# Two decoder blocks on one Trainium2 core: stores of the gate products put in front of the weight loads, reloaded products split earlier, one wait on the last gate narrowed

## The reference

```python
def swiglu_ffn(h, w_in, w_out):
    gate, up = jnp.split(h @ w_in, 2, axis=-1)
    return (jax.nn.silu(gate) * up) @ w_out

# in second_block, FFN_HIDDEN = 2816 = 22 x 128:
h = rms_norm_2(x, pre2_w[l]) * (1.0 + sc2) + sh2
y = swiglu_ffn(h, ffn_w_in[l], ffn_w_out[l])
x = x + (1.0 + gt2) * rms_norm_2(y, post2_w[l])
```

## Time and profile before

| | |
|---|---|
| median of three runs | 2207.89 us (2206.18 to 2208.21) |
| the profiled execution's own time | 2202.16 us |
| its span, first to last instruction | 2200.4 us |
| mean granted clock of TensorE | 0.995 of full speed |
| PE busy | 2147.3 us (98%) |
| POOL, DVE, ACT busy | 1178.6, 1149.8, 710.2 us |
| gate stage | about 1492 to 1632 us of the span |
| unit stage | about 1632 to 1938 us |
| down stage | about 1941 to 2185 us |

### The profile page before, as it was taken

The page is one execution under the profiler, slowest core; times in us unless marked ns, Lnnn a source line. Parts: engine busy times, 40 slices in busy tenths (PEclk is TensorE's granted clock), DMA queues, the critical chain, the costliest instruction groups (busy, mean ns, idle before and its releaser), DMA issues.

```text
span 2200.4 us, 29316 instructions
## 1 busy us (share of the span) xinstructions
PE 2147.3 (98%) x11096; PEld 1743.1 (79%) x11096; DVE 1149.8 (52%) x1413; ACT 710.2 (32%) x878; POOL 1178.6 (54%) x1096
## 2 busy tenths in 40 slices
PE   7999999999999999999999999999999999999997
PEld 5778887887777877787888888887778887878886
DVE  7988873367543261361597246545563343444307
ACT  6663342335433242121222331234432222312112
POOL 3342224566652232222585344566578887857776
PEclk9999999999999999999999999999999999999999
DMA  6224414232421111112233244433754444445343
GB/s 231 87 106 172 172 62 142 73 106 86 162 78 38 68 41 65 55 42 77 87 133 115 97 142 143 162 108 133 261 188 159 151 156 173 174 158 182 134 153 125
DMA packets 93601, 275.16 MB, mean 125 GB/s; under 512 B 8512, under 2 KB 19008, under 8 KB 93504
## 3 DMA queue, kind: packets, MB, share of 16 engines
q1 hardware_dynamic: 81152, 254.97, 32.9%
q10 hardware_dynamic: 12352, 18.88, 2.3%
HBM read 221.38 MB, written 52.43 MB: 124 GB/s over the span
## 4 chain that ended last, share of the span: by engine, by line
PE 85%; DVE 5%; ACT 3%; DMA 2%; issue 1%; DVEq 1%; SPq 1%; POOL 1%; POOLq 1%; ACTq 0%
PE PG L820 37%; PE PG L826 18%; PE PG L1407 13%; PE PG L1321 6%; PE PX L820 2%; PE PX L826 1%; DMA p_gates<-PGB 1%; PE PX L1050 1%; PE PX L1045 1%; PE PG L921 1%; DVE WK L2214 1%; PE PX L1028 1%; PE PX L1065 1%; DVE PX L2220 1%; PE PX L998 0%
## 5 line engine op out<-in xcount | busy, mean ns | idle before, releaser
L820 PE MATMUL PG<-UL,WH 128*128 128x512 f32 x1696 | 662.0, 390 | 0.0
L820 PE MATMUL PG<-UH,WH 128*128 128x512 f32 x1568 | 627.3, 400 | 9.5 <-ACT PGB L2057 5.0
L701 POOL TENSOR_TENSOR TOUCH<-TOUCH 128x2 f32<-128x2 f32 x184 | 55.4, 301 | 837.7 <-PE PG L826 702.3
L704 POOL TENSOR_TENSOR WL<-WRAW,WH 128x1024 fp32r<-128x1024 f32 (+1 forms) x184 | 436.1, 2370 | 30.2 <-issue 30.2
L826 PE MATMUL PG<-UH,WL 128*128 128x512 f32 x1568 | 400.5, 389 | 0.0
L820 PEld LDWEIGHTS PG<-UL,WH 128*128 128x128 f32 x1696 | 319.1, 188 | 67.9 <-issue 4.1
L820 PEld LDWEIGHTS PG<-UH,WH 128*128 128x128 f32 x1568 | 294.9, 188 | 89.0 <-issue 14.6
L826 PEld LDWEIGHTS PG<-UH,WL 128*128 128x128 f32 x1568 | 294.4, 188 | 61.7
L702 POOL TENSOR_SCALAR WH<-WRAW 128x1024 fp32r<-128x1024 f32 (+1 forms) x184 | 188.6, 1025 | 0.0
L1407 PE MATMUL PG<-TH,AH 128*128 128x512 f32 x352 | 137.9, 392 | 8.2 <-DVE U L3129 4.6
L1407 PE MATMUL PG<-TL,AH 128*128 128x512 f32 x352 | 137.5, 391 | 0.0
(11 more groups left out here) (584 smaller groups left out, 3857.9 us busy)
## 6 DMA issues: line engine op xcount, KB each, us to landing
ADA<-ada_w SPq DMA_DIRECT2D x24, 1024.0 KB, 5.1
W2RAW<-down_w SPq DMA_DIRECT2D x48, 512.0 KB, 3.3
RAW<-up_w SPq DMA_DIRECT2D x22, 1024.0 KB, 7.1
WRAW<-out_w SPq DMA_DIRECT2D x30, 512.0 KB, 3.2
WRAW<-zg_w SPq DMA_DIRECT2D x24, 512.0 KB, 3.2
gates<-STG ACTq DMA_DIRECT2D x24, 512.0 KB, 2.6
WK<-gates SPq DMA_DIRECT2D x24, 512.0 KB, 3.3
WRAW<-up_w SPq DMA_DIRECT2D x22, 512.0 KB, 3.6
```

What stands on the lines that cost most here:

```text
L701: pool.tensor_tensor(TOUCH[:, 0:2], TOUCH[:, 2:4], TOUCH[:, 4:6], ALU.add)
L704: pool.tensor_tensor(WL[:, r, 0:n], WRAW[:, r, 0:n], WH[:, r, 0:n].bitcast(F32), ALU.subtract).then_inc(w_split, 1)
L820: mm = pe.matmul(out, w[:, r, at + P * k:at + P * k + P], v, start=first and k == ks[0] and n == 0, stop=False)
```

## The change

SP's order in the gate stage goes by single tiles: the store of tile 2i - 4 + j is issued in front of the load of tile 2i + j (j = 0, 1), where before both stores came behind both loads. The reads of `hidden` rows 0 to 5 are issued behind unit 9 (before: unit 15), those of rows 6 to 9 behind unit 11 (before: unit 15), those of rows 10 to 13 behind unit 15 (before: unit 16). ACT waits for rows 0 to 5 behind unit 14 and splits them behind units 14 to 19; DVE makes their low parts behind units 15 to 20. To have room for that the hardware loops of SP, ACT and DVE are shorter and more units are written out. At the head of the unit stage PE waits for the SiLU of tile 20 in place of tile 21, and for that of tile 21 only in front of the third block product, the first that writes a bank of tile 21. No arithmetic is added or removed.

```diff
-            def gate_pair(i):
-                for j in range(2):
-                    sp.wait_ge(w_split, 2 * i + (TILE0["gate_up"] + j - 1))
-                    sp.dma_start(WRAW[:, j, :], dram["up_w"][4 * i + 2 * j]).then_inc(w_loaded[j], 16)
+            def gate_tile(i, j):
+                sp.wait_ge(w_split, 2 * i + (TILE0["gate_up"] + j - 1))
+                sp.dma_start(WRAW[:, j, :], dram["up_w"][4 * i + 2 * j]).then_inc(w_loaded[j], 16)
...
             for i in range(11):
-                gate_pair(i)
-                for n in (2 * i - 4, 2 * i - 3) if i >= 2 else ():
-                    p1_out(n)
+                for j in range(2):
+                    if i >= 2:
+                        p1_out(2 * i - 4 + j)
+                    gate_tile(i, j)
...
-            with sp.Fori(0, 7) as i:
+            with sp.Fori(0, 4) as i:
...
-            unit_moves(15, 1)
-            sp.wait_ge(values_saved[0], SAVED0 + 32 * 8)
-            sp.wait_ge(values_saved[1], SAVED0 + 32 * 7 + 16)
-            hidden_in(0, 0, 6, UHF[:, 0:6, 0:512], 4)
-            hidden_in(0, 6, 4, UHF[:, 0:4, 512:1024], 0)
-            unit_moves(16, 0)
-            hidden_in(0, 10, 4, ULF[:, 0:4, 512:1024], 0)
-            for i in range(17, UNITS - 2):
+            def all_saved(n):
+                sp.wait_ge(values_saved[0], SAVED0 + 32 * ((n + 1) // 2))
+                sp.wait_ge(values_saved[1], SAVED0 + 32 * (n // 2) + 16)
+
+            for i in range(9, UNITS - 2):
                 unit_moves(i, i % 2)
+                if i == 9:
+                    all_saved(9)
+                    hidden_in(0, 0, 6, UHF[:, 0:6, 0:512], 4)
+                if i == 11:
+                    hidden_in(0, 6, 4, UHF[:, 0:4, 512:1024], 0)
+                if i == 15:
+                    all_saved(15)
+                    hidden_in(0, 10, 4, ULF[:, 0:4, 512:1024], 0)
...
-            pe.wait_ge(ffn_silu, N_HIDDEN)
+            pe.wait_ge(ffn_silu, N_HIDDEN - 1)
             with pe.Fori(0, UNITS) as i:
...
                 block_product(i, S3, PG[:, 1, :], t_block(3))
+                pe.wait_ge(ffn_silu, N_HIDDEN)
                 block_product(i, S1, PG[:, 2, :], t_block(1))
...
-            with act.Fori(0, 7) as i:
+            with act.Fori(0, 6) as i:
...
-            unit(15, 1)
-            act.wait_ge(hidden_loaded[4], LOADED0[4] + 16)
-            for i in range(16, UNITS - 1):
+            for i in range(13, UNITS - 1):
                 unit(i, i % 2)
-                split_hidden(0, i - 16)
+                if i == 14:
+                    act.wait_ge(hidden_loaded[4], LOADED0[4] + 16)
+                if 14 <= i < 20:
+                    split_hidden(0, i - 14)
             high_last(UNITS - 1)
             gate_second(UNITS - 2)
-            split_hidden(0, 5)
             gate_second(UNITS - 1)
...
-            with dve.Fori(0, 8) as i:
+            with dve.Fori(0, 6) as i:
                 for p in range(2):
                     join_unit(i * 2 + p, p)
-            for i in range(16, UNITS):
+            for i in range(12, UNITS):
                 join_unit(i, i % 2)
-                split_low(0, i - 16)
+                if 15 <= i < 21:
+                    split_low(0, i - 15)
```

## The result

The changed kernel takes 2178.13 us (median of 4 runs, 2177.31 to 2178.85) beside 2207.95 us (2206.18 to 2208.21) for the kernel before: 0.9867 of its time [0.9849, 0.9884], a gain of 29.8 us where 24.5 were forecast. It is faster, and in the places named, but by 5.3 us more than the sum. Its profiled execution has its own time of 2178.8 us, a span of 2177.1 us and a mean granted clock of 0.997.

A forecast was written before the change was run, and what follows sets the result against it. The prediction took TensorE's matmuls plus PE's waits as the bound: 25.9 us of waits less rests of 1.0 and 0.4 gives 24.5, so 2207.89 - 24.5 = 2183.4 us, range 2180 to 2190 (8 in 10: 2179.5 to 2192).

The forecast's parts named there:

- the five places: PE's waits: five gate tiles 6.4 us, tile 8's sum 4.35, unit stage head 3.9, unit 16 6.4, down stage head 4.8.
- Stores in front of loads: Gate stage: stores are ready 1.7 us before loads, so waits at tiles 4, 14, 18, 20 and tile 8's sum go.
- the chain of DVE and ACT: Gate stage, tiles 14 to 20: cost 0; as rival it sets the pace (33.8 us against 32.7), gain 20, 2188, chance 0.06.
- the one of late landings: Rival, gate stage: stores issued early still land late, taking 7.66 us; gain 16.7 us, time 2191, chance 0.13.
- The loop that would have made the kernel slower: Rival, gate stage: late SiLU, load, split and tile feed each other; 27 us lost, time 2210, chance 0.04.
- Tile 10: Gate stage: behind the eight stores of H a wait of 1.0 us (0 to 2.3) was to remain.
- the window given: Gate stage: the store of tile 6, issued behind the eight stores of H, lands at 1549.5 to 1551 us.
- The rival that kept the wait and let the clock fall there: Gate stage, tile 10: PE stands 2.3 us plus 1.6 for the clock, rest 3.9 us; time 2186.3, chance 0.17.
- The narrowed wait: Head of the unit stage: the 3.9 us wait shrinks to a rest of 0.4 us (0 to 1.3).
- the 0.05 us of the bound: Unit stage, S1: the wait repeated in 22 units costs 0, at most 22 x 0.05 = 1.1 us.
- The rows: Rows read sooner: unit 16's 6.4 us and the down stage head's 4.8 us go, rest 0 (bound 0.5).
- I carry the difference to the median: Final sum: the profiled execution's 5.7 us below the median stays, so 24.5 is taken from 2207.89, not 2202.16.

The follow-up runs named there:

- the first trace: The kernel before, unchanged, in its first profiled execution: 2202.16 us.
- a_again: The changed kernel with no edit, run and profiled again on another chip: 2177.70 us, 0.9875 of before.
- p_rows: The kernel before with only the loops, reads and splits of the hidden rows changed: 2193.28 us, 0.9940 of before.
- l_norows: The changed kernel with the reads of hidden rows, their splits and the hardware loops put back as before: 2188.16 us, 0.9918 of before.
- b_look2: The kernel before, unchanged, one more profiled execution: 2205.53 us.
- b_again: The kernel before, unchanged, run and profiled again: 2205.59 us, 0.9995; its profiled execution 2206.61 us.
- b_look1: The kernel before, unchanged, one more profiled execution: 2205.50 us.

## Why the prediction was right, and where it was not

*What bounds the kernel, and the five places*: right. Every wait named is gone, and by the table above each is worth its term to 0.4 us, but for tile 10. Three of the terms hold a price for the clock, and the first trace has the fall at each: 0.50 for 3.4 us from 1545.5, 1862.9 and 1941.4 us, at waits of 2.48, 4.64 and 2.92 us.

*Stores in front of loads*: right. Store ready before load, no wait on a DMA but at tile 8, tiles 14, 18 and 20 without a wait, so the chain of DVE and ACT with its 33.8 us for six tiles did not show: that rival falls, and the one of late landings too (a median of 2.8 us, where it needed 7.66). The loop that would have made the kernel slower has no sign in the trace.

*Tile 10*: a rest of 1.0 us was taken, 0 was found (0.58 in a_again). The store of tile 6 went out at 1544.33 and let ACT go at 1550.58, which looks like the window given (1549.5 to 1551). But this trace runs 1.65 us late from its start: on the forecast's scale ACT went at 1548.9, 0.6 us ahead of the window, and so it did in a_again (1548.86). The term that was too large is the time for which the eight hold SP, 10.3 us in the forecast, 8.8 and 8.7 in these two traces. ACT's table load, which the 2.5 us behind the store contain, took 1.28 us in the traces of before and after. PE reached tile 10 at 1553.89, 0.8 us behind the SiLU's end at 1553.09, and on that scale at 1552.2, as forecast (1552.1). The rival that kept the wait and let the clock fall there did not happen in either trace of the changed kernel.

*The narrowed wait*: the mechanism was right, 0.3 us of rest for 0.4, and the wait in S1 costs nothing: from 1640 to 1800 us the matmuls of both kernels keep their distance to 0.01 us (a wait's record on PE's queue is 51 ns long in the trace of before, beside the 0.05 us of the bound). Its size was off: 3.9 us was the price in the one execution of before where the clock held. In 7 of the 9 traces of kernels in which PE waits there for the last SiLU, unfilled (3.6 or 2.7 us), the clock fell behind it (0.50 for 3.4 us in six, for 6.8 us in p_rows), and the price was 1.4 to 1.6 us more in six of the seven and 2.7 us more in p_rows.

*The rows*: right to 0.1 us against the first trace (11.3 us by start times for 11.2; the median landing of the 48 loads of the down weights there is 3.3 us, the lower end taken for the third tile's); 10.5 us by l_norows.

*The step that failed* is "That one was 5.7 us below the median of the runs, and I carry the difference to the median". It treats the distance as a property of the program that no edit touches, and so prices each wait by the execution in which the clock held. The traces show that about half of it belongs to the waits: behind 1500 us the three other executions lose 3.7, 3.4 and 1.6 us against the first, 2.9 us in the mean, of which 1.6 at the head of the unit stage in each and 1.2 to 1.5 from tile 4 to tile 11 in two. The change takes these waits away, and the losses with them: the changed kernel's profiled execution is 0.7 us above the median of its runs, not 5.7 below, and its eight runs of two comparisons lie within 1.5 us, where the first four of before spread over 2.0 and 15 on one chip over 5.6 (more runs spread more for that alone). So the traces give 24.9 + 2.9 = 27.8 us (the mean of the two sums of the changed kernel, and that of the three of before; 27.1 if the first trace is counted as a fourth), and 27.6 was measured beside a_again.

The 5.3 us by which the first comparison beat the sum are then 0.4 us of the terms themselves (24.9 for 24.5), 2.9 us of the carried difference, and 2.0 us that no trace shows: its four runs of before have a median of 2207.95, where before took 2205.3 to 2207.0 in the four later groups of runs. Whether that is the chip or chance is open.

The profile had the hint: the clock fell behind 2.48 us at tile 8 and behind 2.92 us (0.50 for 3.4 us each), yet not behind the 3.6 us at the unit stage (1.00 from 1632 to 1640 us). So the length of a wait alone did not say whether the clock falls, and the prediction priced the 3.6 us as if its luck were a rule.

## What to carry to other kernels

Where TensorE waits long enough for its clock to fall (here that was seen from 2.48 us on, with a granted clock of 0.50 for 3.4 or 6.8 us), price the wait with and without the fall (here 1.4 to 1.6 us in six of seven traces), and don't take from one trace which it is: look at each such wait, and count the ones where the clock held as luck that the next execution may not have. When the profiled execution stands well off the median, ask which of its waits were lighter; if the change removes them, the difference is gained and not carried. Where a wait can't be removed, a few useless matmuls in it can bring the clock's part back (here 0.6 and 2.4 us by five of them at one place).

## What the runs showed of the hardware that was not expected

- 32 useless matmuls in the waits made the kernel 5.0 us faster; five at one place gave 0.6 us in one pair of four runs each and 2.4 us in another.
- Whether the clock falls behind a wait of 2.48 us (tile 8, twice in four traces of before), 2.7 or 3.6 us differs between executions of one program; where it fell there in the traces of before it was 0.50 for 3.4 us. Behind 4.3 to 5.0 us (unit 16) it fell in all four traces of before, to 0.50 for 3.4 us in two (before, b_look2) and for 6.8 us in two (b_again, b_look1).
- The first 20 us differ too. The opening matmuls in the changed kernel's first trace, and then in a_again:

```profile
15.29 0.63 PE L960 MATMUL PG<-UH,WH 128*128 128x512 f32 x1
15.72 0.63 PE L960 MATMUL PG<-UL,WH 128*128 128x512 f32 x1
...
18.28 0.43 PE L960 MATMUL PG<-UL,WH 128*128 128x512 f32 x1
```

```profile
14.21 0.40 PE L960 MATMUL PG<-UL,WH 128*128 128x512 f32 x1
14.44 0.40 PE L960 MATMUL PG<-UH,WL 128*128 128x512 f32 x1
```

They start every 0.43 us at first and every 0.23 us later; the change of pace came at 18.3 us in the one and at 13.7 us in the other, which is the 1.65 us ahead of the change. The granted clock reads 1.00 in both from 8 to 24 us, so only the starts of the matmuls show it.
- A store of 512 KB lands in 2.8 us when issued by itself and in 5.1 us when issued in pairs (medians of the gate stage, after and before); behind the eight stores of H it took 6.2 us as the first (after) and 7.7 and 8.1 us as the third (before, b_again).
